# Expert rows summed in DRAM by accumulating DMAs, with the last tile placed by TensorE

## The reference, cut to what matters

```python
h2 = rms_norm(x, lp['g_norm2']) * (1 + sc2) + sh2
x = x + gt2 * moe(h2, lp['w_router'], lp['b_router'], lp['w_gate'], lp['w_up'], lp['w_down'])
```

## Time and profile before

| | us |
|---|---|
| Median of 3 runs | 1660.75 |
| Lowest and highest run | 1660.02, 1660.82 |
| Profiled execution, own time given as its span | 1665.8 |
| PE busy in it | 1550.5 |
| DVE busy in it | 899.4 |
| ACT busy in it | 700.1 |
| POOL busy in it | 297.8 |

### The profile page before, as it was taken

One profiled execution on the slowest core, in us unless ns is written; L12 is line 12 of the kernel. 1 busy time (PEld: TensorE's weight loads), 2 busy tenths in 40 slices (PEclk: granted clock), 3 DMA queues, 4 the chain that ended last, 5 costly groups with the idle time before them and its releaser, 6 DMA issues.

```text
span 1665.8 us, 21787 instructions
## 1 busy us (share of the span) xinstructions
PE 1550.5 (93%) x8180; PEld 1107.1 (66%) x8180; DVE 899.4 (54%) x1723; ACT 700.1 (42%) x1335; POOL 297.8 (18%) x321
## 2 busy tenths in 40 slices
PE   4999999999999989999779999999999999899992
PEld 1777777777787855554456777777777888555561
DVE  1566664455554752455575656543455556344554
ACT  4543554445521313444553455534454132144550
POOL 1001000011101014565200010000111010345640
PEclk9999999999999989999989999999999999999996
DMA  8541205534365379999847212353345253898847
GB/s 339 205 153 58 77 26 189 185 109 161 111 234 219 135 278 400 383 401 346 303 178 270 95 39 77 120 185 126 114 152 204 87 202 127 308 414 336 331 143 286
DMA packets 92376, 337.55 MB, mean 203 GB/s; under 512 B 20960, under 2 KB 21024, under 8 KB 89328
## 3 DMA queue, kind: packets, MB, share of 16 engines
q1 hardware_dynamic: 53136, 197.68, 32.5%
q0 software_dynamic: 38992, 135.86, 22.1%
q10 hardware_dynamic: 144, 2.62, 0.4%
HBM read 351.22 MB, written 47.35 MB: 239 GB/s over the span
## 4 chain that ended last, share of the span: by engine, by line
PE 81%; DMA 8%; DVE 6%; ACT 2%; issue 2%; SPq 1%; POOL 0%; POOLq 0%; ACTq 0%; DVEq 0%
PE ps L1884 16%; PE ps L1886 16%; PE ps L1885 16%; PE ps L2214 6%; PE ps L1876 5%; DMA gu_b<-w_gu,eidx 4%; PE ps L2263 3%; PE ps L2036 3%; PE ps L2018 2%; PE ps L1843 2%; PE ps L1792 2%; PE ps L2096 2%; PE ps L2197 2%; PE ps L2230 2%; PE ps L2070 1%
## 5 line engine op out<-in xcount | busy, mean ns | idle before, releaser
L1884 PE MATMUL ps<-hi,hT_hi 128*128 128x512 f32 x960 | 392.8, 409 | 5.5 <-ACT o_a L1094 3.0
L1886 PE MATMUL ps<-hi,hT_lo 128*128 128x512 f32 x960 | 377.1, 393 | 0.0
L1885 PE MATMUL ps<-lo,hT_hi 128*128 128x512 f32 x960 | 376.3, 392 | 0.0
L1884 PEld LDWEIGHTS ps<-hi,hT_hi 128*128 128x128 f32 x960 | 181.8, 189 | 64.8 <-issue 23.6
L1886 PEld LDWEIGHTS ps<-hi,hT_lo 128*128 128x128 f32 x960 | 181.4, 189 | 40.1
L1885 PEld LDWEIGHTS ps<-lo,hT_hi 128*128 128x128 f32 x960 | 182.2, 190 | 32.4
L890 ACT ACTIVATE hi<-raw 128x1024 fp32r<-128x1024 f32 x106 | 108.4, 1054 | 136.6 <-DMA raw<-w_stream 136.6
L1236 DVE TENSOR_TENSOR lo<-raw,hi 128x1024 fp32r<-128x1024 f32 x106 | 127.5, 1220 | 65.4 <-ACT hi L890 65.0
L1715 DVE TENSOR_TENSOR lo<-raw,hi 128x1024 fp32r<-128x1024 f32 x96 | 112.7, 1221 | 39.7 <-ACT hi L1161 33.9
L2214 PE MATMUL ps<-gu_a,xT 128*64 128x512 f32 x256 | 116.1, 607 | 6.7 <-DMA gu_b<-w_gu,eidx 6.7
L2214 PE MATMUL ps<-gu_b,xT 128*64 128x512 f32 x256 | 116.1, 607 | 0.0
(11 more groups left out here) (312 smaller groups left out, 2880.8 us busy)
## 6 DMA issues: line engine op xcount, KB each, us to landing
raw<-w_stream SPq DMA_DIRECT2D x112, 512.0 KB
raw<-w_gu SPq DMA_DIRECT2D x80, 512.0 KB
raw_m<-w_stream SPq DMA_DIRECT2D x68, 512.0 KB, 5.4
raw<-w_dn SPq DMA_DIRECT2D x40, 512.0 KB
bias_na<-na_bias POOLq DMA_DIRECT2D x32, 384.0 KB, 3.4
sg<-sg_d POOLq DMA_DIRECT2D x8, 1280.0 KB, 9.7
y<-ye_d SPq DMA_DIRECT2D x20, 512.0 KB, 5.2
raw_p<-w_stream SPq DMA_DIRECT2D x16, 512.0 KB, 16.0
```

The lines of the kernel that those rows point to most:

```text
L1884: pe.matmul(out, w_hi, m_hi, start=first, stop=False)
L1885: pe.matmul(out, w_hi, m_lo, start=False, stop=False)
L1886: return pe.matmul(out, w_lo, m_hi, start=False, stop=last)
```

## The change

There is no ye_d and no x_spill for the experts any more. x is parked in an accumulator in DRAM, acc[l][0], which has 640 rows for the tokens and 128 spare ones. A second accumulator, acc[l][1], is zeroed by five DMAs from a tensor of zeros, issued on POOL between the gate stores of the attention. For every tile but the last, `add_rows` writes the tile's rows with an indirect DMA that adds to what stands in DRAM. Places without a token are added to the spare rows, so all 128 places are always written. A pair tile takes two such DMAs of 64 rows, one into each accumulator; full tiles alternate. An add waits until the one before it into the same accumulator has landed. After the adds of tile 14, `join` adds acc[l][1] to acc[l][0] with one DMA from DRAM to DRAM. The adds of tiles 15 and 16 go to acc[l][0]; that of tile 15 waits for the join.

The rows are scaled by gt2 before they are stored: SP loads both gt2 rows early (gtm), `row_gates(n)` on DVE picks the row of each place, and `ys(n)` is now two DVE operations that multiply the PSUM half by the weight and by that row. ACT has no part in it. For the last tile, DVE builds five 128x128 placement matrices (`last_places`), PE multiplies them with ysb (ten matmuls of 128x512), and DVE adds the result to x tiles loaded from acc[l][0] (`last_rows`, two operations of 512 columns for each token tile). The head of the second layer is reordered on ACT and DVE, and PE's filler matmuls ahead of it are gone. The descriptor memory for POOL's DMAs is set to 8192.

```diff
-                    for t in range(NT):
-                        for j, dst in enumerate((Y1[t], Y2[t])):
-                            r0 = (j * NT + t) * P
-                            sp.dma_start(dst[:], ye_d[r0:r0 + P, :]).then_inc(gathered[t].sem, 16)
+                    sp.wait_ge(added[0].sem, added[0].at(l, N_ADDS[0] - 1))
+                    for t in range(NT):
+                        sp.dma_start(x[:, t, :], acc_x[l][:, t, :]).then_inc(x_loaded[t].sem, 16)
...
+LAST = MOE_TILES - 1
+SETTLED = LAST - 2
+    ADD_TO[_n, 0] = SCHED[_n][1] % 2 if IS_FULL[_n] and _n < SETTLED else 0
+    if not IS_FULL[_n]:
+        ADD_TO[_n, 1] = 1
...
+                sp.wait_ge(mod_stored.sem, mod_stored.at(l, 3))
+                for cond in range(2):
+                    sp.dma_start(gtm[:, cond, :], mod_d[l, cond, 5 * D:6 * D].partition_broadcast(P)
+                                 ).then_inc(gtm_loaded.sem, 16)
...
+                    if 2 <= g < 2 + NT:
+                        r0 = (g - 2) * P
+                        po.dma_start(acc[l][1][r0:r0 + P, :], zero_in).then_inc(settled.sem, 16)
...
+                def add_part(n, h):
+                    b = ADD_TO[n, h]
+                    if ADD_NO[n, h] >= 1:
+                        po.wait_ge(added[b].sem, added[b].at(l, ADD_NO[n, h] - 1))
+                    rows_at = row_h if h else row_i
+                    p1 = P if IS_FULL[n] else HALF
+                    po.indirect_dma_start(acc[l][b], bass.IndirectOffsetOnAxis(rows_at[0:p1, XD_COL[n]:XD_COL[n] + 1], 0),
+                                          ysb[n % 2][h * HALF:h * HALF + p1, :], None, bounds_check=ACC_ROWS - 1,
+                                          oob_is_err=True, compute_op=ALU.add).then_inc(added[b].sem, 16)
...
+                    if n == 0:
+                        po.wait_ge(x_parked.sem, x_parked.at(l, 0))
+                        po.wait_ge(settled.sem, settled.at(l, NT - 1))
+                    if n == SETTLED:
+                        po.wait_ge(settled.sem, settled.at(l, NT))
                     po.wait_ge(y_dve.sem, y_dve.at(l, n))
-                    po.indirect_dma_start(ye_d, bass.IndirectOffsetOnAxis(row_i[:, XD_COL[n]:XD_COL[n] + 1], 0),
-                                          ysb[n % 2][:], None, bounds_check=2 * NT * P - 1,
-                                          oob_is_err=False).then_inc(y_stored[n % 2].sem, 16)
+                    for h in range(1 if IS_FULL[n] else 2):
+                        add_part(n, h)
+
+                def join():
+                    po.wait_ge(added[0].sem, added[0].at(l, ADD_NO[SETTLED, 0] - 1))
+                    po.wait_ge(added[1].sem, added[1].at(l, N_ADDS[1] - 1))
+                    po.dma_start(acc[l][0][0:NT * P, :], acc[l][1][0:NT * P, :], accum_op=ALU.add,
+                                 max_dma_last_dim=4 * D).then_inc(settled.sem, 16)
...
-                def ys(n):
-
-                    act.wait_ge(*down_done(l, n))
-                    if n >= 2:
-                        act.wait_ge(y_stored[n % 2].sem, y_stored[n % 2].at(l, n // 2 - 1))
...
-                    act.activation(ysb[n % 2][:, 0:512], ps[:, 2, :], ACT.Copy, scale=w_slot[:, c:c + 1]).then_inc(y_act.sem, 1)
...
-                def mix_rows(l, t):
-                    dve.wait_ge(gathered[t].sem, gathered[t].at(l, gathered[t].n - 1))
-                    after(chained(dve.tensor_tensor(Y1[t][:], Y1[t][:], Y2[t][:], ALU.add)))
...
+                def last_rows(l, t):
+                    dve.wait_ge(x_loaded[t].sem, x_loaded[t].at(l, 0))
+                    dve.wait_ge(pm_done.sem, pm_done.at(l, t))
+                    for j in range(2):
+                        half_row = x[:, t, 512 * j:512 * j + 512]
+                        ins = dve.tensor_tensor(half_row, ps[:, PERM_BANKS[t][j], :], half_row, ALU.add)
+                    ins.then_inc(x_ready.sem, 1)
...
+                def row_gates(n):
+                    if n >= 2:
+                        for h in range(1 if IS_FULL[n - 2] else 2):
+                            b = ADD_TO[n - 2, h]
+                            dve.wait_ge(added[b].sem, added[b].at(l, ADD_NO[n - 2, h]))
...
+                    return chained(STT(out=ysb[n % 2][:], in0=gtm[:, 0, :], scalar=p_slot[:, c:c + 1], in1=gtm[:, 1, :],
+                                       op0=ALU.mult, op1=ALU.add))
...
+                    if n >= 1:
+                        gated = row_gates(n - 1)
                     dve.wait_ge(silu_done.sem, silu_done.at(l, n))
                     dve.tensor_tensor(hid[:], ps[:, 0, D_EXP:2 * D_EXP], silu_g[:], ALU.mult).then_inc(hid_done.sem, 1)
...
+            def last_places(l, t):
+                if t == 0:
+                    pe.wait_ge(y_dve.sem, y_dve.at(l, LAST))
+                if t >= 3:
+                    pe.wait_ge(x_ready.sem, x_ready.at(l, t - 3))
+                for j in range(2):
+                    if t == 0:
+                        pe.wait_ge(y_dve.sem, y_dve.at(l, LAST + 1 + j))
+                    ins = pe.matmul(ps[:, PERM_BANKS[t][j], :], perm[:, t, :], ysb[LAST % 2][:, 512 * j:512 * j + 512],
+                                    start=True, stop=True)
+                ins.then_inc(pm_done.sem, 1)
...
-                            keep_busy(8, 4)
+                            for t in range(3):
+                                last_places(l - 1, t)
                             head_rows_in(l, 0)
-                            keep_busy(5, 4)
+                            last_places(l - 1, 3)
+                            last_places(l - 1, 4)
```

More of the change, by code:

```diff
@@ L75 @@
 PAIR_AT = [n for n in range(MOE_TILES) if not IS_FULL[n]]
+LAST = MOE_TILES - 1
+SETTLED = LAST - 2
+ACC_ROWS = (NT + 1) * P
+ADD_TO = {}
+for _n in range(LAST):
+    ADD_TO[_n, 0] = SCHED[_n][1] % 2 if IS_FULL[_n] and _n < SETTLED else 0
+    if not IS_FULL[_n]:
+        ADD_TO[_n, 1] = 1
+ADD_NO = {key: sum(1 for other in ADD_TO if other < key and ADD_TO[other] == b) for key, b in ADD_TO.items()}
+N_ADDS = [sum(1 for b in ADD_TO.values() if b == a) for a in range(2)]
 XD_COL = [n if kind == "full" else N_FULL + n for kind, n in SCHED]
 FULL_USES = N_FULL // 2
+PERM_BANKS = [(0, 1), (4, 7), (2, 3), (0, 1), (4, 7)]
 SLOT_USES = [sum(1 for u in range(NU) if u % SLOTS == s) for s in range(SLOTS)]
@@ L476, in program @@
         ht_lo = Signal("ht_lo", sum(IS_SPLIT))
[L477 to L480, removed]
+        y_dve = Signal("y_dve", LAST + 3)
+        added = [Signal(f"rows_added{b}", N_ADDS[b], 0, 16) for b in range(2)]
+        settled = Signal("acc_zeroed_joined", NT + 1, 0, 16)
+        gtm_loaded = Signal("gtm_loaded", 2, 0, 16)
+        pm_done = Signal("pm_done", NT)
+        x_loaded = [Signal(f"x_loaded{t}", 1, 0, 16) for t in range(NT)]
         x_ready = Signal("x_ready", NT)
@@ L671, in _ @@
                 sp.wait_ge(x_ready.sem, x_ready.at(DEPTH - 1, t))
-                sp.dma_start(y_out[:, t, :], x[:, t, :]).then_inc(s_out, 16)
-            sp.wait_ge(s_out, 16 * NT)
+                sp.dma_start(y_out[:, t, :], x[:, t, :]).then_inc(x_parked.sem, 16)
+            sp.wait_ge(x_parked.sem, x_parked.layer * DEPTH + 16 * NT)
         @blk.gpsimd
@@ L863, in _ @@
                     if n >= 2:
-                        store_rows(n - 2)
+                        add_rows(n - 2)
+                    if n - 2 == SETTLED - 1:
+                        join()
                     if n - 2 in PAIR_AT[:-2]:
@@ L1013, in _ @@
                     head_xn(0)
+                    head_square(1)
                     for t in range(NT):
@@ L1751, in _ @@
                     head_rows(l + 1)
+                dve.wait_ge(gtm_loaded.sem, gtm_loaded.at(l, 1))
+                after(chained(TT(gtm[:, 0, :], gtm[:, 0, :], gtm[:, 1, :], ALU.subtract)))
                 for n in range(MOE_TILES):
```

151 lines of the change are left out of this document (80 added, 71 removed).

## The result

The changed kernel takes 1729.97 us (median of 4 runs, 1723.8 to 1735.7) against 1660.78 of the kernel before on the same chip: ratio 1.041, 95% interval 1.038 to 1.045. The forecast was 1652.5, its range ended at 1678: wrong in sign and far outside the range. The profiled execution has a span of 1721.9 us against 1665.8, so 56.1 us can be placed in the profile. The medians are 69 us apart: the changed kernel's profiled execution was its fastest (6.2 us under the median), and about 13 us of the difference can't be placed in any stretch.

What follows compares the result with a forecast made beforehand. PE bounds the kernel (busy 93%, 81% of the last chain), with full DMA queues in the experts. End -12, passage -6 and experts +10 make -8: 1652.7 against the median of 1660.75, put at 1652.5, range 1640 to 1678.

Steps and rivals of the forecast that it cites:

- the new waits costed at nothing: Experts: POOL's waits for earlier adds, up to 10 us, cost nothing; 3 to 5 us each if the queue ran dry.
- The experts' +10: Inside the experts: dearer adds ahead of weight gathers delay three of them by 3.3 us each; ends +2 and +35.
- three late gu_b: Experts: the three weight gathers PE waited for in the old profile, landing 19.7 to 22.8 us after issue.
- 0.32 taken: Assumed price in us of adding one 4 KB packet, twice a copy; ends 0.16 and 0.58.
- The end's -12: End of layer 2: last x at 1652 instead of 1662.8, 11 us gained, 12 with loads partly ahead.
- The named end of +1: End of layer 2: the slow end of that term's range, +1 us with the dear add; the other end was -17.
- The passage's -6: Between the layers: pitch of 9.5 us a tile falls to about 8, against a later join; ends -10 and +5.
- +2, -8 and +1: Between the layers: 2 us lost by the join chain, 8 gained by pitch and faster start, 1 lost to lower clock.
- signs named beforehand: Wrong if: add packet over 0.35 us in full queue, PE's experts waits up over 20 us, or pitch still 9.5 us.
- Full queues decide, slower: Rival, experts: adds at 0.37 to 0.58 a row or POOL's waits leaving the queue dry; 1672 to 1700; 33%.
- The gain is only moved: Rival, end: join and two serial adds take as long as the old passes, join over 22 us; 1661; 8%.
- A free add: Rival: adding costs only a copy's price, -25 us in sum, so 1636; 12%.

Runs made afterwards that it cites:

- e12a: The kernel before plus ten zero fills of 512 KB a layer into a rows tensor for each layer, still overwriting: 1664.2 us.
- e12b: The kernel before plus the same ten zero fills a layer, its 18 row stores a layer adding instead of overwriting, no wait added: 1684.8 us.
- e14: The changed kernel with four accumulator tensors and four row buffers instead of two each, and unused places skipped; gates left out of the output: 1690.2 us.
- e8: The changed kernel with four accumulator tensors and four row buffers instead of two each, unused places still added; gates left out of the output: 1709.0 us.
- e3: The changed kernel with four accumulator tensors instead of two, so an add waits for the one four adds before it: 1711.6 us.
- e5_no_join: The changed kernel without the join; the last two tiles' adds no longer wait for it, and the second tensor's rows are left out: 1697.1 us.
- e6: The changed kernel with four buffers of finished rows instead of two; the gates and their operation are left out: 1722.4 us.
- e10: The kernel before with ScalarE's half of the row scaling moved to VectorE, nothing else of the change: 1661.7 us.
- e4: The changed kernel with unused places out of bounds and skipped instead of added to spare rows: 1717.5 us.
- e2: The changed kernel with scattered rows overwriting instead of being added; waits, zero fills and join stay: 1690.5 us.

## Why the prediction was wrong

**The experts' loss in terms.** The runs give a ladder from the kernel before (with fills) to the one after, by experts of layers 1 and 2. Adding instead of storing, at the same rows and waits: +8.6, +8.7 (e12a to e12b). Other buffers and order: +1.4, -0.1 (e14). The unused places as added rows: +9.8, +5.5 (e14 to e8). The waits for earlier adds: +6.0, +7.7 (e8 to after). Sum 25.8 and 21.8, which is what lies between 187.6 and 213.4, and 183.4 and 205.2. The terms depend on the order: with the waits in place, skipping the places gives back only 0.4 and 1.0. So each delay is partly hidden by another, and none alone is the cause. The last term is the least certain: it also holds the gates' operation, which e8 leaves out, and e8 and the changed kernel are 12 us apart by their profiled spans and 21 by their medians.

**The step that failed first: the new waits costed at nothing.** "I cost this at nothing: what it waits for is in the same queue with up to 1.5 MB (4 us) behind it, so the queue does not run dry." This reasoned about the queue's throughput, and PE waits for single landings. POOL stood 98 us in its waits for earlier adds of rows, seven and four times. Four tensors alone gave 18 us back (e3), four tensors and four buffers 21 (e8). The same paragraph named the way that the delay took (row_gates ahead of hid, "and that can hold PE") and gave it no number; PE lost 16 and 14 us there. The 18 us are 1.7 for each of the eleven waits: less than the "3 to 5 us" that the paragraph had for them if the queue ran dry, but more than the whole gain of 8 that was forecast, so this term alone turns its sign. It is not the whole miss of 77 us; the other terms follow.

**The experts' +10, measured +44.** With the waits taken out (14 by the ladder) some 30 are left, which the sum had at 10. The sum counted three late gu_b, since these were the waits of the kernel before. It was the wrong list: with dearer adds it is xg and dn_b that arrive late too (e12b), and in the kernel after gu_b had only 2.6 us of waits. It also left out what PE loses at a lower granted clock beside its waits, 5.0 and 3.4 us in e12b. A row's price in full queues was near: 0.35 us for 0.32 taken; overwriting instead takes 0.18 less, 0.17 (0.16 in the earlier trace rows). The Trainium skill's rule of half the rate for an inline add ("Collectives: The Full Stack", section on why ReduceScatter is half of AllGather) is borne out by the join: 0.34 us a packet is 2.1 times the plain store's 0.16. The lone scattered rows, at 0.42, are 2.6 times. The price in full queues was not what failed; what it was multiplied by was.

**The end's -12, measured +2 (from down(17)) or +4 (from hid).** Counted from the end of down(17), the forecast had x complete after 16.2 us and it was 28.6. The join was 4 us later than forecast: it was issued 2.5 later, and took 16.5 instead of 15 us. The two adds took 6.9 us from issue to issue and 6.4 to landing, not 4 and 4.5: 4.7 us; a lone added packet costs 0.42 us and eight of them stand in a row on each engine. The x loads and what follows took 12.2 us, not 8.5. The sum is 12.4 us late. The named end of +1 was near. DVE's ten operations are 0.69 us each, as forecast. The 3.7 us behind the loads are PE's: the forecast had all ten products beside the DMAs, at 0.44 us each from the earlier trace rows. But the 16 entries there are records, and a product of f32 stands as two (one tile's eight products are 16 records), so it is 0.88 us; and the last two tiles can be placed only when banks come free, behind the first loads. Their four products, 8 records, took 5.41 us at the granted clock of 0.68, and 3.70 at the same place in e5_no_join, where PE had stood for 1.7 us. That the last tile's rows "need only the last tile's ysb" was wrong too, since that buffer waits for tile 15's add; e6 shows that this cost nothing here.

**The passage's -6, measured +9.** (Its parts, +2, -8 and +1, make -5.) The pitch came as forecast, 9.5 to 7.7. The join did not: forecast to land at 827, it was issued only at 841.45. The experts themselves ended 24 us later (last hid at 842.2 for 818.1), and tile 14's second add was issued 7 us behind its first, after a wait of 4.98 us, and took 8.2 us to land. Then 19.1 us passed to tile 15's add, 6.9 to tile 16's and 6.4 to its landing. PE stood 19.7 us with nothing, and the clock granted from 860 to 870 us was 0.50 of full speed, the lower of its two levels. e5 shows both: without the join the passage is 7.4 us shorter than before, where the forecast without its 2 us for the join is -7 or -8. So this term was right but for the join in its way.

**What was right.** VectorE's longer rows (e10: 0), the fills (e12a: about 2 us for twice as many), the pitch, and the price of a packet. Of the signs named beforehand, PE's waits are over their limit of 20 us (29.7 for hid alone), a packet's price stands at its limit of 0.35 us.

**The rivals.** "Full queues decide, slower" at 1672 to 1700 had the sign and the place, and 33%, and the time lies beyond even its far end. Its mechanism holds in part. Rows of 0.35 us in full queues cost 17 us in the experts of the kernel before (e12b), and the unused places 15 us more where no wait hides them (e14), but about 1 where the waits stand (e4). The same rival had POOL's waits only as a queue that runs dry; the queues did not (shares of 0.99 and 0.92 in the two layers' experts), and the waits cost time all the same. "The gain is only moved" had the end within 2 to 4 us, though not by the join of over 22 us that it asked for: the join took 16.5, and the serial adds and PE's placing did the rest. A free add is ruled out by 0.34 us a packet. A rival with POOL's waits at the 3 to 5 us that the text itself gave would have stood at 1686 to 1708, nearer, but by a price that e3 does not bear out.

**What stays open.** e8 has no wait for an earlier add, yet its first layer's experts are 4 us longer than with four tensors alone; no run tells why. How much of PE's lower clock follows from the waits alone was not tried. Nor was a rule found that leads from 0.18 us a row in the queues to the delay of each gather. And about 13 us of the 69 lie between the profiled executions and the medians.

## What to carry to other kernels

A wait is costed by what waits behind it on its engine and by the landing of a single transfer, not by the throughput of the queue: adds of 64 or 128 rows, some 3 us of data or less at 0.34 to 0.42 us a packet, landed 10.5 us after their issue (median of 34), and whatever waited for one waited for that. A mean share of the queues over a whole stage hides the steps in which they are full; read it in windows. Count matrix products by the program, not by the records of the trace. Where a step gets dearer, do not scale only the waits that the old profile shows; ask which transfers share its queue, all of them. Before trading VectorE passes (15 of 1.22 us, at each layer's end) for DMAs that add, count the chain of landings that takes their place: here 16.5 + 6.9 + 6.4 + 3.9 us.

## What the runs showed of the hardware

- A DMA that adds costs an engine 0.34 us (join, DRAM to DRAM) to 0.42 us (lone scattered rows) a packet of 4 KB against 0.16 for a plain store; in busy queues it was 0.35 (e4), and 0.18 to 0.19 less when it overwrote instead (e12b against e12a, e2 against the kernel after).
- A lone add of 128 scattered rows of 4 KB lands 6.4 us after its issue; in the kernel after, the first or only add of a tile landed after 10.5 us (median of 34), the second add of a pair tile (64 rows) after 6.2 (median of 14).
- Changing nothing but the kind of 36 stores of rows cost 20.6 us of 1664, with the queues at 0.96 or more of their time for most of the experts.
- Places that are out of bounds move no data in an indirect DMA: skipping 1887 rows of 4 KB took 7.73 MB and 653 us of engine time off the queue.
- An f32 product of 128x128 and 128x512 stands as two records in the trace, 0.88 us at full clock (16 records in 7.01 us).
